# A permuted table for the ranks within a block of a mixture-of-experts layer

## The chip, the cores and the metric

The kernel runs on one core of a Trainium2 chip. The metric is the device time of one execution in microseconds (us). The core has TensorE (PE), VectorE (DVE), ScalarE (ACT), GpSimd (POOL) and SyncE (SP), and 16 DMA engines that move data between the chip's memory (HBM) and the on-chip SBUF.

## The reference

Two transformer blocks on 512 tokens of width 1024, in float32. The change touches only the last sublayer, a mixture of 32 experts of which each token takes two. Cut to that:

```python
weights = p_grp[:, None] * top_p / jnp.sum(top_p, axis=-1, keepdims=True)
expert_id = grp[:, None] * EXPERTS_PER_GROUP + top_e
...
order = jnp.argsort(flat_e)
...
def run_block(args):
    xb, e, wb = args
    a = jax.nn.silu(xb @ w_gate[e]) * (xb @ w_up[e])
    return (a @ w_down[e]) * wb[:, None].astype(xb.dtype)
...
y = jnp.zeros((T, D), h.dtype).at[slot_tok].add(out.reshape(cap, D))
```

The 1024 pairs of token and expert (512 tokens, `TOP_K` 2) are grouped by expert; each expert's rows go through gate, up and down; the results are added back to their tokens. In which order the rows of one expert stand does not matter to the result.

## The kernel before

The program runs the first transformer block, the second block's mixer, and then the routing and the experts. One instruction stream for each engine is written out by hand, with semaphores between them.

**Routing** (VectorE, lines 2010 to 2099). For each pair the kernel computes a slot: a block number and a rank within a block of `BS` = 64. The first 64 tokens of expert e go to block e (32 blocks), the rest of experts with more than 64 tokens to overflow blocks after them. `dst_r` is the rank, `dst_b` the start of the block. Two one-hot tables are made by comparison: `block_tok` (line 2077, block against all blocks, then multiplied by the token's number) and `place` (line 2079, rank against the table `iota_r`, which holds 0 to 63). TensorE multiplies the two (line 2790), so that row p, column b of the product says which token stands on partition p of block b; the same matmul is done for both halves of 64 partitions. From it come `slot_i`, the index of the row to gather, and `pair_i`, the index of the row to scatter to. A spot with no token gets an index out of bounds.

```python
dve.tensor_tensor(place, cols(tab3, TAB3, "iota_r").unsqueeze(1).to_broadcast([P, 8, BS]),
                  dst_r.unsqueeze(2).to_broadcast([P, 8, BS]), ALU.is_equal).then_inc(S("places_ready"), 1)
```

**The experts.** For each block b, GpSimd gathers up to 64 rows of 4 KB from `xn_rows` in HBM into 64 partitions of `raw` (`gather`, line 865, four blocks ahead). TensorE turns them (line 2818), VectorE scales and shifts them (lines 2107, 2109), TensorE computes gate and up (`gate_up`, line 2802, 32 matmuls), ScalarE and VectorE form the activation (lines 1300 to 1308, 2114, 2116), TensorE turns it and computes down (`down`, line 2810), VectorE multiplies the result (line 2123), and GpSimd scatters it to `y_rows` in HBM (`scatter`, line 870). A result row of 4 KB is scattered as two rows of 2 KB, since `down` leaves its left half on partitions 0 to 63 and its right half on 64 to 127: 128 rows in each scatter. The order on TensorE is: gate_up(b), turn and down of b - 1, rows of b + 2.

```python
pool.indirect_dma_start(xg(v), None, xn_rows, bass.IndirectOffsetOnAxis(ap=index, axis=0),
                        bounds_check=T - 1, oob_is_err=False).then_inc(S(f"xg_loaded{v}"), 16)
```

**The weights** (SP, `expert_gu` line 627 with 2 MB for gate and up, `expert_dn` line 631 with 1 MB for down) go into seven slots. The load of block b + 7 is issued when gate_up(b), or down(b), is done. The two overflow blocks take the same way in a loop at the end (lines 728 and 731). After the last scatter SP loads `y_rows` (line 742), and the four tiles of 128 tokens are summed, normed and stored.

**Tables.** `routing_tables` (lines 1979 to 1988) prepares constants on VectorE between the two halves of the output projection, where it follows the operations of lines 1997 and 1999.

Of the kernel before, what the change touches and what calls it, by code (L numbers as in the profile page):

```python
# [26 lines left out]
P = 128  # L27
# [41 lines left out]
BS = 64  # L69
# [34 lines left out]
def columns(fields):  # L104
    at, out = 0, {}
    for name, n in fields:
        out[name] = (at, at + n)
        at += n
    out["_"] = (0, at)
    return out  # L110
# [5 lines left out]
TAB3 = columns([("dec", 32), ("iota", NBLK), ("thr", 8), ("tok", 2 * NT), ("iota_r", BS), ("iota_b", NBLK + 2), ("final_g", D)])  # L116
# [162 lines left out]
def build(nc, x, wp, par_d, con_d, smw_d, bias_d, par2_d, smw2_d, tab2_d, tab3_d, wexp, out):  # L279
    with ExitStack() as ctx:  # L280
# [5 lines left out]
        def S(name):  # L286
            if name not in sems:
                sems[name] = ctx.enter_context(nc.semaphore(name))
            return sems[name]
# [32 lines left out]
        def AR(a, n):  # L322
            return arena[:, a:a + n]

        def cols(t, table, name):
            a, b = table[name]
            return t[:, a:b]
# [149 lines left out]
        tab3 = AR(14848, TAB3_N)  # L477
# [3 lines left out]
        def AT(n):  # L481
            at[0] += n
            assert at[0] <= 18560
            return AR(at[0] - n, n)
# [21 lines left out]
        place = AR(12288, 8 * BS).rearrange("p (c n) -> p c n", c=8)  # L506
# [6 lines left out]
        half_of = AT(1)  # L513
        dst_i = AT(8).bitcast(I32)
        idxc, idxp = AT(WS).bitcast(I32), AT(WS).bitcast(I32)
        nblkf = AT(1)
        nblk_i = AT(1).bitcast(I32)
        actf = AT(2 * P).rearrange("p (u n) -> p u n", u=2)
# [24 lines left out]
        def wait_group(eng, what, i):  # L543
            eng.wait_ge(S("group_filled"), GIDX[what, i] + 1)
            return BANKS[WHERE[GIDX[what, i]]]
# [787 lines left out]
        def _(dve):  # L1333
            c = [0]

            def own(ins):
                c[0] += 1
                ins.then_inc(S("dve_step"), 1)
                dve.wait_ge(S("dve_step"), c[0])
# [64 lines left out]
            for c4 in range(4):  # L1404
                b = wait_group(dve, "cT", c4)
# [228 lines left out]
            for t in range(len(units) + 3):  # L1634
# [14 lines left out]
                if t == len(units) + 1:  # L1649
                    b = wait_group(dve, "csq", 0)  # L1650
# [46 lines left out]
            for r in range(FQ):  # L1697
                for j in range(4):
                    if m < MOD_PIECES:
                        mod_part(m)  # L1700
                    for f in range(2):
                        i = (r * 4 + j) * 2 + f
# [7 lines left out]
                for j in range(4):  # L1710
# [15 lines left out]
                    for t in range(NT if j % 2 else 0):  # L1726
                        i = (r * 2 + half) * 4 + t
                        xt = Xv[:, t, half * 512:(half + 1) * 512]
                        b = wait_group(dve, "down", i)
# [40 lines left out]
            b = wait_group(dve, "if", 0)  # L1770
            free_group(dve.tensor_copy(if_rows, b[0:8, :]), "if", 0)
            b = wait_group(dve, "ifT", 0)
# [7 lines left out]
            b = wait_group(dve, "lb", 0)  # L1780
# [26 lines left out]
            b = wait_group(dve, "cum", 0)  # L1807
# [3 lines left out]
            for h in range(MH):  # L1811
                b = wait_group(dve, "crow", h)
# [63 lines left out]
            for i in range(8):  # L1876
                b = wait_group(dve, "bm", i)
# [8 lines left out]
            for f in range(5):  # L1886
                b = wait_group(dve, "cT2", f)
# [17 lines left out]
            b = wait_group(dve, "krT", 0)  # L1905
# [3 lines left out]
            for t in range(NT):  # L1909
                b = wait_group(dve, "qr", t)  # L1910
# [8 lines left out]
            for t in range(NT):  # L1919
                b = wait_group(dve, "qrT", t)  # L1920
# [29 lines left out]
            for t in range(len(aunits) + 5):  # L1950
# [6 lines left out]
                if t >= 11 and (t - 11) % 8 < 2:  # L1957
                    q, i = divmod(t - 11, 8)
                    b = wait_group(dve, "yaT", 2 * q + i)
# [7 lines left out]
            for i in range(8):  # L1967
# [4 lines left out]
                b = wait_group(dve, "ba", i)  # L1972
# [6 lines left out]
            def routing_tables():  # L1979
                dve.wait_ge(S("tables_loaded"), TABLES["tab3"])  # L1980
                dve.tensor_copy(tri_r, cols(con, CON, "tri"))
                dve.tensor_copy(one_r, one.to_broadcast([P, 2]))
                dve.tensor_scalar(second[:, 0:4], cols(tab3, TAB3, "tok")[:, 0:4], -8.0 * T, None, ALU.add)
                dve.tensor_scalar(second[:, 4:8], cols(tab3, TAB3, "tok")[:, 4:8], -7.0 * T, None, ALU.add)
                dve.memset(half_of[0:BS, :], 16.0 * T)
                dve.memset(half_of[BS:P, :], 16.0 * T + 1)
                dve.memset(slot_i.bitcast(F32), float(T))
                dve.tensor_tensor(triex[0:32, :], cols(con, CON, "tri")[0:32, 0:32], ident[0:32, 0:32], ALU.subtract)

            wait_freed(dve, "g1r", 1)  # L1990
            dve.wait_ge(S("x_back"), 16)
            for half in range(2):
                for t in range(NT):
                    i = 4 * half + t
                    b = wait_group(dve, "wout", i)
                    w = wtmp[:, i % 2, :]
                    own(dve.tensor_tensor(w, b[:, :], g1row[:, half * 512:(half + 1) * 512], ALU.mult))
                    xt = Xv[:, t, half * 512:(half + 1) * 512]
                    free_group(dve.tensor_tensor(xt, xt, w, ALU.add), "wout", i)
                if half == 0:  # L2000
                    routing_tables()
# [3 lines left out]
            for n in (5, 7):  # L2005
                b = wait_group(dve, "xT", n)
# [15 lines left out]
            b = wait_group(dve, "gr", 0)  # L2022
            free_group(dve.tensor_copy(gr_rows[0:100, :], b[0:100, 0:256]), "gr", 0)
            b = wait_group(dve, "grT", 0)
# [27 lines left out]
            b = wait_group(dve, "cnt", 0)  # L2052
# [4 lines left out]
            b = wait_group(dve, "rank", 0)  # L2057
            free_group(dve.tensor_tensor(Sl, b[:, 0:128].rearrange("p (t n) -> p t n", t=NT), Aa.bitcast(F32), ALU.subtract), "rank", 0)
            b = wait_group(dve, "pstart", 0)
# [8 lines left out]
            for A, k in ((A1, 0), (A2, 1)):  # L2068
# [7 lines left out]
            iota_b = cols(tab3, TAB3, "iota_b").unsqueeze(1).to_broadcast([P, 8, NBLK + 2])  # L2076
            own(dve.tensor_tensor(block_tok, iota_b, dst_b.unsqueeze(2).to_broadcast([P, 8, NBLK + 2]), ALU.is_equal))
            own(dve.tensor_tensor(block_tok, block_tok, second.unsqueeze(2).to_broadcast([P, 8, NBLK + 2]), ALU.mult))
            dve.tensor_tensor(place, cols(tab3, TAB3, "iota_r").unsqueeze(1).to_broadcast([P, 8, BS]),
                              dst_r.unsqueeze(2).to_broadcast([P, 8, BS]), ALU.is_equal).then_inc(S("places_ready"), 1)  # L2080
            b = wait_group(dve, "slots", 0)
            own(dve.tensor_scalar(slot_f[:, 0:NBLK + 2], b[:, 0:NBLK + 2], -7.0 * T, -float(T), ALU.is_ge, ALU.mult))
# [54 lines left out]
            with dve.Fori(0, OVER // WS) as i:  # L2137
                for v in range(WS):
                    b, u = NE + WS * i + v, v % 2
# [901 lines left out]
```

## Time and profile before

| | |
|---|---|
| Time, median of 3 runs | 1604.31 us (1603.09 to 1606.16) |
| The profiled execution, its own time | 1599.82 us |
| Its span, first to last instruction | 1598.0 us |
| Granted TensorE clock, mean | 0.981 |
| Busy: PE, DVE, ACT, POOL | 1503.4, 782.5, 454.9, 588.3 us |
| DMA over the whole span | 260.92 MB, mean 163 GB/s |

How to read the profile: times are microseconds from the start of the span unless marked ns. PE is TensorE's matmuls and PEld its weight loads. Busy is the time in which an engine executes. The DMA share is the mean busy share of the 16 DMA engines (measured packet by packet, so it can come out a little above 1), and GB/s is what they moved. "issue" as a releaser means that the engine waited for nothing that the profile shows. A transfer is cut into packets; queue q1 holds the plain loads and stores that SP issues, q0 the gathers and scatters that GpSimd issues. The completion of a transfer is itself one small packet on each of the 16 engines.

### The profile page before, as it was taken

The numbers are of one execution on the slowest core, as the hardware profiler recorded it, in microseconds if no ns is written. First come the engines' busy times: TensorE is split into PE (matmuls) and PEld (weight loads), VectorE is DVE, ScalarE is ACT, GpSimd is POOL, SyncE is SP. The second block draws the span as 40 slices with busy tenths as digits, with TensorE's granted clock in tenths as the row PEclk, the third lists the DMA queues.
The fourth block names the chain that finished last, engine by engine and source line by source line (L and its number), as shares of the span: only waits on it lengthen the run. The fifth ranks groups of instructions, "written<-read, shape, count | busy, mean of one in ns | idle before, by whom it ended". The sixth has DMA issues, their size and how long they took to land.

```text
span 1598.0 us, 21257 instructions
## 1 busy us (share of the span) xinstructions
PE 1503.4 (94%) x8338; PEld 1188.7 (74%) x8338; DVE 782.5 (49%) x1490; ACT 454.9 (28%) x734; POOL 588.3 (37%) x486
## 2 busy tenths in 40 slices
PE   7999999999999999999999999999999989977885
PEld 6978887878888888877888988775788766544442
DVE  5475657387786863245605602445313354432334
ACT  4342334342222313252414332442223211100001
POOL 5551222434545444553533154510254313321222
PEclk9999999999999999999999999999999999988898
DMA  4250110335445442222322022310143799999995
GB/s 174 104 199 27 53 54 1 132 132 199 170 179 190 182 161 105 105 113 79 112 79 80 27 83 102 115 54 1 43 169 139 302 354 365 370 397 367 394 409 208
DMA packets 37348, 260.92 MB, mean 163 GB/s; under 512 B 7280, under 2 KB 7920, under 8 KB 13184
## 3 DMA queue, kind: packets, MB, share of 16 engines
q1 hardware_dynamic: 31488, 251.13, 41.4%
q0 software_dynamic: 5760, 8.41, 1.7%
q8 instruction: 68, 1.11, 0.3%
q14 instruction: 32, 0.26, 0.0%
HBM read 252.69 MB, written 17.30 MB: 169 GB/s over the span
## 4 chain that ended last, share of the span: by engine, by line
PE 83%; DVE 6%; issue 5%; ACT 2%; POOL 2%; DMA 1%; DVEq 0%; SPq 0%; ACTq 0%; POOLq 0%
PE G L2214 13%; PE G L2216 12%; PE G L2215 12%; PE SA L2802 4%; PE G L2802 4%; PE SA L2214 3%; PE SA L2216 3%; PE SA L2215 3%; PE PB L2216 3%; PE PB L2215 3%; PE PB L2214 3%; PE OB L2411 2%; POOL wl L770 1%; PE PB L2810 1%; PE SA L2682 1%
## 5 line engine op out<-in xcount | busy, mean ns | idle before, releaser
L770 POOL TENSOR_TENSOR wl<-raw,wh 128x512 fp32r<-128x512 f32 x352 | 476.3, 1385 | 676.0 <-ACT wh L925 666.3
L925 ACT ACTIVATE wh<-raw 128x2048 fp32r<-128x2048 f32 x90 | 172.3, 1914 | 270.9 <-PE SA L2216 142.6
L2214 PE MATMUL G<-Hh,wh 128*128 128x512 f32 x544 | 216.4, 398 | 2.6 <-DVE arena L1617 1.4
L2216 PE MATMUL G<-Hh,wl 128*128 128x512 f32 x544 | 212.8, 391 | 0.0
L2215 PE MATMUL G<-Hl,wh 128*128 128x512 f32 x544 | 212.4, 391 | 0.0
L1694 DVE SCALAR_TENSOR_TENSOR arena<-arena,st 128x256 f32<-128x256 f32 x144 | 132.9, 923 | 5.1
L2214 PEld LDWEIGHTS G<-Hh,wh 128*128 128x128 f32 x544 | 102.5, 188 | 23.4 <-issue 2.2
L2216 PEld LDWEIGHTS G<-Hh,wl 128*128 128x128 f32 x544 | 102.4, 188 | 22.2
L2215 PEld LDWEIGHTS G<-Hl,wh 128*128 128x128 f32 x544 | 102.6, 189 | 19.5
L865 POOL DMA_INDIRECT raw<-xn_rows,arena x38 | 36.6, 963 | 131.2 <-PE G L2818 107.5
L2214 PE MATMUL G<-wh,Hh 128*128 128x256 f32 x256 | 77.6, 303 | 1.1 <-POOL wl L770 1.0
L2216 PE MATMUL G<-wh,Hl 128*128 128x256 f32 x256 | 72.9, 285 | 0.0
L2215 PE MATMUL G<-wl,Hh 128*128 128x256 f32 x256 | 72.9, 285 | 0.0
L2214 PE MATMUL G<-Yh,wh 128*128 128x512 f32 x168 | 65.6, 390 | 1.6 <-DVE Yl L1890 1.6
L870 POOL DMA_INDIRECT y_rows<-arena x34 | 34.4, 1013 | 87.2 <-DVE arena L2123 82.3
L1011 ACT ACTIVATE arena<-arena,st 128x128 f32<-128x128 f32 (+3 forms) x64 | 35.9, 561 | 103.8 <-DVE st L1576 103.8
L2216 PE MATMUL G<-Yh,wl 128*128 128x512 f32 x168 | 65.4, 389 | 0.0
L2215 PE MATMUL G<-Yl,wh 128*128 128x512 f32 x168 | 65.4, 389 | 0.0
L1585 DVE COPY arena<-PB 128x128 f32<-128x128 f32 (+3 forms) x64 | 31.3, 489 | 49.2 <-PE PB L2401 48.8
L2214 PE MATMUL SA<-wh,Yh 128*128 128x512 f32 x134 | 53.6, 400 | 0.0
L2214 PEld LDWEIGHTS G<-wh,Hh 128*128 128x128 f32 x256 | 49.4, 193 | 4.1 <-issue 1.7
L2216 PE MATMUL SA<-wh,Yl 128*128 128x512 f32 x134 | 52.4, 391 | 0.0
(535 smaller groups left out, 3087.4 us busy)
## 6 DMA issues: line engine op xcount, KB each, us to landing
raw<-in_pieces_dram SPq DMA_DIRECT2D x91, 1024.0 KB, 4.8
arena<-in_pieces_dram SPq DMA_DIRECT2D x24, 1024.0 KB, 4.8
arena<-in_wexp_dram SPq DMA_DIRECT2D x11, 2048.0 KB
dn_w<-in_wexp_dram SPq DMA_DIRECT2D x18, 1024.0 KB
arena<-in_wexp_dram SPq DMA_DIRECT2D x12, 1024.0 KB, 26.9
gu_y<-in_wexp_dram SPq DMA_DIRECT2D x6, 2048.0 KB
gu_z<-in_wexp_dram SPq DMA_DIRECT2D x5, 2048.0 KB, 43.3
gu_h<-in_wexp_dram SPq DMA_DIRECT2D x4, 2048.0 KB, 37.1
```

The costliest lines, as they stand in the source:

```text
L770: ins = pool.tensor_tensor(low_[:, part], whole[:, part], high[:, part], ALU.subtract)
L865: pool.indirect_dma_start(xg(v), None, xn_rows, bass.IndirectOffsetOnAxis(ap=index, axis=0), bounds_check=T - 1, oob_is_err=False).then_in ...
L870: pool.indirect_dma_start(y_rows, bass.IndirectOffsetOnAxis(ap=index, axis=0), yb[:, u, :], None, bounds_check=4 * T - 1, oob_is_err=False ...
L925: act.activation(split_pair(s)[0], wait_raw(act, sp_list[s]), ACT.Copy).then_inc(S("high_split"), 1)
L1011: act.activation(SP[:, u % 2, 0:nk], SP[:, u % 2, 0:nk], ACT.Exp, scale=-1.0, bias=nmax[:, u % 2:u % 2 + 1], accum_out=rsum[:, ((u // 8) % ...
L1585: dve.tensor_copy(PTs[:, u % 2, 0:nk], PB[u % 2][:, 0:nk]).then_inc(S("pt_copied"), 1)
L1694: own(dve.scalar_tensor_tensor(a, w[:, k, :], condc[:, k:k + 1], a, ALU.mult, ALU.add))
L2214: pe.matmul(out, ah, bh, start=first, stop=False)
L2215: pe.matmul(out, ah, bl, start=False, stop=False)
L2216: return pe.matmul(out, al, bh, start=False, stop=last)
L2411: ins = pe.matmul(OB[:, h * HD:(h + 1) * HD], PTs[:, u % 2, k * P:(k + 1) * P], Zv[:, k, ty, (h // 4) * HD:(h // 4 + 1) * HD], start=k == ...
L2802: ins = pe.matmul(GU[u][BS * j:BS * j + BS, 0:256], xgT[:, u, k, :], wg[:, j, k, :], start=k == 0, stop=k == KT - 1)
```

## The change

A second table of 64 numbers, `rank_at`, is built once from `iota_r` and takes its place in the comparison that makes `place`. It holds a permutation of 0 to 63: with a rank written in bits as (b, c, j, i), where i has three bits and the others one each, the rank stands at position (c, i, j, b). So ranks 0 to 7 stand at positions 0, 4, 8, ... 28; ranks 8 to 15 at 2, 6, ... 30; ranks 16 to 31 at the even positions from 32 on; and ranks 32 to 63 at the odd ones. A token of rank r is then found at that partition of its block, in the gather and in the scatter alike. Nothing else is changed.

```diff
@@ -513,6 +513,7 @@
         half_of = AT(1)
         dst_i = AT(8).bitcast(I32)
         idxc, idxp = AT(WS).bitcast(I32), AT(WS).bitcast(I32)
+        rank_at = AT(BS)
         nblkf = AT(1)
         nblk_i = AT(1).bitcast(I32)
         actf = AT(2 * P).rearrange("p (u n) -> p u n", u=2)
@@ -1985,6 +1986,11 @@
                 dve.memset(half_of[0:BS, :], 16.0 * T)
                 dve.memset(half_of[BS:P, :], 16.0 * T + 1)
                 dve.memset(slot_i.bitcast(F32), float(T))
+                ranks = cols(tab3, TAB3, "iota_r").rearrange("p (b c j i) -> p b j c i", b=2, c=2, j=2)
+                spots = rank_at.rearrange("p (c i j b) -> p b j c i", c=2, j=2, b=2)
+                for j in range(2):
+                    for b in range(2):
+                        dve.tensor_copy(spots[:, b, j], ranks[:, b, j])
                 dve.tensor_tensor(triex[0:32, :], cols(con, CON, "tri")[0:32, 0:32], ident[0:32, 0:32], ALU.subtract)
 
             wait_freed(dve, "g1r", 1)
@@ -2076,7 +2082,7 @@
-            dve.tensor_tensor(place, cols(tab3, TAB3, "iota_r").unsqueeze(1).to_broadcast([P, 8, BS]),
+            dve.tensor_tensor(place, rank_at.unsqueeze(1).to_broadcast([P, 8, BS]),
                               dst_r.unsqueeze(2).to_broadcast([P, 8, BS]), ALU.is_equal).then_inc(S("places_ready"), 1)
```

On VectorE the four copies stand behind the constants of `routing_tables`, in the middle of the output projection (`arena` is the large work area, `con` the constants, SA and PB banks of PSUM). Before:

```order
L1987 MEMSET arena 128x52
L1988 TENSOR_TENSOR arena<-con 32x32
L1997 TENSOR_TENSOR arena<-SA,arena 128x512
L1999 TENSOR_TENSOR X<-X,arena 128x512
```

And now:

```order
L1988 MEMSET arena 128x52
L1993 COPY arena<-arena 128x16 x4
L1994 TENSOR_TENSOR arena<-con 32x32
L2003 TENSOR_TENSOR arena<-SA,arena 128x512
L2005 TENSOR_TENSOR X<-X,arena 128x512
```

Four copies of 16 elements on 128 partitions are new; the rest keeps its order, six lines further down in the file. No other engine has an instruction more or less.

## Rows read from the trace of the kernel before

**Rows 1.** Chain that ended last, gate and up: start us, us, what.
```profile
1354.22 3.45 PE G L2802 x32
1360.30 3.45 PE SA L2802 x32
...
1537.25 3.67 PE G L2802 x32
1544.98 3.67 PE SA L2802 x32
1553.88 3.47 PE G L2802 x32
```

**Rows 2.** Stretches: us, busy of PE, PEld, DVE, ACT, POOL, PEclk, DMA share, GB/s.
```profile
1350.00:1380.00 30.00, 29.91 (x250) 18.42 (x248) 14.12 (x25) 3.27 (x10) 9.86 (x10) 1.00 1.01 381
...
1500.00:1530.00 30.00, 22.15 (x154) 13.41 (x156) 9.13 (x17) 1.96 (x6) 6.93 (x7) 0.87 1.01 402
1530.00:1550.00 20.00, 18.26 (x144) 11.17 (x142) 5.91 (x11) 1.96 (x6) 2.99 (x3) 0.94 1.00 418
```

**Rows 3.** PE line 2802 from 1390 to 1546: idle before it, by releaser (us, times).
```profile
  issue: 29.1, 13
```

**Rows 4.** Stretches of 2 us at the end of the weight stream.
```profile
1556.00:1558.00 2.00, 2.00 (x23) 1.44 (x18) 0.14 (x1) 0.38 (x1) 0.98 (x4) 1.00 0.92 383
1558.00:1560.00 2.00, 0.94 (x8) 0.59 (x8) 1.90 (x4) 0.28 (x1) 0.70 (x1) 1.00 0.78 322
1560.00:1562.00 2.00, 2.00 (x14) 0.99 (x12) 0.40 (x2) 0.00 (x0) 0.00 (x0) 1.00 0.53 215
1562.00:1564.00 2.00, 2.00 (x22) 1.60 (x20) 0.47 (x1) 0.00 (x0) 0.67 (x1) 1.00 0.42 174
1564.00:1566.00 2.00, 1.90 (x20) 1.25 (x15) 0.38 (x1) 0.38 (x1) 0.34 (x1) 1.00 0.35 131
1566.00:1568.00 2.00, 1.04 (x7) 0.68 (x9) 1.84 (x4) 0.28 (x1) 0.00 (x0) 1.00 0.17 70
1568.00:1570.00 2.00, 1.39 (x8) 0.25 (x4) 0.47 (x1) 0.00 (x0) 0.31 (x2) 1.00 0.13 41
1570.00:1572.00 2.00, 0.00 (x0) 0.00 (x0) 0.22 (x1) 0.00 (x0) 0.99 (x1) 1.00 0.00 0
```

**Rows 5.** Stretches of 1 us at the end of the y_rows loads.
```profile
1587.00:1588.00 1.00, 1.00 (x4) 0.30 (x2) 0.96 (x2) 0.00 (x0) 0.91 (x2) 1.00 0.56 229
1588.00:1589.00 1.00, 0.37 (x1) 0.00 (x0) 0.84 (x1) 0.59 (x3) 0.92 (x2) 1.00 0.02 8
```

**Rows 6.** DMA queues and issues of the whole program: packets, MB; issues.
```profile
q0 software_dynamic: 5760, 8.41, 1.7%
...
raw<-xn_rows,arena POOLq DMA_INDIRECT x38
y_rows<-arena POOLq DMA_INDIRECT x34
```

**Rows 7.** DMA packets from 1502.3 to 1503.1 (two rows), then to 1506.0.
```profile
DMA packets 51, 0.32 MB, mean 405 GB/s; under 512 B 19, under 2 KB 19, under 8 KB 26
q0 software_dynamic: 25, 0.03, 11.4%
...
q0 software_dynamic: 80, 0.03, 3.7%
```

**Rows 8.** DVE in order of time: start us, us, line, operation, [idle before].
```profile
1251.82 0.16 DVE L1984 TENSOR_SCALAR arena<-arena 128x4 f32<-128x4 f32 x1
...
1264.08 0.69 DVE L1997 TENSOR_TENSOR arena<-SA,arena 128x512 f32<-128x512 f32 x1 [11.79 <-PE SA L2216]
...
1294.94 0.69 DVE L2079 TENSOR_TENSOR arena<-arena 128x512 f32<-128x512 f32 x1
```

**Rows 9.** Chain that ended last: the first gather.
```profile
1298.35 4.54 DMA raw<-xn_rows,arena
```

**Rows 10.** DMA packets from 1315 to 1545.
```profile
DMA packets 12059, 87.89 MB, mean 382 GB/s; under 512 B 3722, under 2 KB 3722, under 8 KB 5515
```

## The prediction

> **What bounds the kernel now.** I read the busy shares by stretch first, then the chain, then the DMA views. The stage that matters is the expert loop, from about 1307 us to the end: 32 blocks of 64 ranks, one for each expert, then two overflow blocks. The reader should see four things.
>
> The loop has two paces. Early, the gate-and-up groups follow each other at 1354.22, 1360.30 us: 6.08 us a block, with TensorE busy throughout [rows 1, 2]. Late they start at 1537.25, 1544.98 and 1553.88: 7.7 us and more [rows 1], and TensorE is busy only 22.15 of 30 us [rows 2]. From 1390 to 1546 it stands idle 29.1 us ahead of these groups for nothing that the profile shows [rows 3]. The group waits for rows, for a free buffer and for its weights. The first two come from engines that the view would name; what is left is the weight load.
>
> The DMA engines are busy all the time: share 1.01 in both paces and 1.00 up to 1550 [rows 2]. So the stream of weights sets the late pace, and what counts is when the last gate-and-up load (block 31) is complete.
>
> A load is complete when the slowest of its 16 engines is done, and the engines are far from each other. At the end of the stream the share falls 0.92, 0.78, 0.53, 0.42, 0.35, 0.17, 0.13 over windows of 2 us from 1556 on [rows 4]. That is one engine after another running dry, over 14 us. The sum is 3.30, so the mean engine ends 6.6 us after 1556, and the last near 1570, 14 us after it: **the slowest is 7.4 us behind the mean**. The y_rows loads later, with no row transfers among them, end sharply: 0.56, then 0.02 a microsecond later [rows 5]. So the engines are not unequal as such. Something between 1300 and 1556 drove them apart.
>
> **What drives them apart.** The only transfers there that need not be even are the gathers and the scatters: 38 and 34, 8.41 MB [rows 6]. Absent ranks are skipped: 1024 assignments of 4 KB, gathered and scattered, are just 8.39 MB. Packets tell how rows are laid out. The gather of block 31, with 8 tokens, is 80 packets: 64 rows and 16 completions. Its packets between 512 B and 8 KB number 26 less 19, that is 7, in the first 0.8 us [rows 7]; at most one more can follow. The whole program has 5760 such packets [rows 6]. 38 x 64 gathered rows, 72 x 16 completions and 34 x 128 scattered rows would be 7936; with scattered rows in twos it is 2432 + 1152 + 2176 = 5760, exactly. Rows that share a packet share an engine, so neighbouring ranks do lie together, and low ranks, which nearly every expert has, load always the same engines. The single packet records, which no view groups, fit twos for the gather and fours for the scatter (low half rows on one set of eight engines, high half rows on the other).
>
> The reference's routing gives the tokens of each expert: 5 to 89, two of them above 64. With that placement I added up bytes by engine. Before, the heaviest engine has 252 KB more than the mean over all 34 blocks, and 219 KB when block 31's weights land (32 gathers, 28 scatters). With permuted ranks it has 72 and 65 KB.
>
> **The change part by part.**
> - Four copies of 128x16 on VectorE. The nearest rows are 0.16 us for 128x4 and 0.69 us for 128x512 [rows 8]; I take 0.2 us each, 0.8 us in all. They stand where VectorE is then idle for 11.79 us, waiting for TensorE [rows 8]. Even at 0.69 each, 2.8 us are covered. Cost: 0. Without that cover it would be the 0.8.
> - The comparison reads another table of the same shape: 0.69 us as now [rows 8]. Cost: 0.
> - The same 1024 ranks are matched, so bytes, numbers of transfers, of turns on GpSimd and of matmuls stay. The first gather, 4.54 us on the chain [rows 9], has 25 tokens: at most two rows per engine either way. Cost: 0; I keep 0.3 us to either side.
> - Evenness of the engines. An engine moves 418/16 = 26.1 GB/s [rows 2]. 252 KB are then 9.7 us, where the decline shows 7.4: the trace gives 0.77 of the arithmetic. At block 31 the lead of the heaviest falls by 219 - 65 = 154 KB, 5.9 us, times 0.77: **-4.5 us**. The ends are 0 (the skew has another cause) and -7.4 (perfect evenness). I take 4.5, since it is held to the decline.
> - Scattered rows. The even spots now hold ranks 0 to 31 and the odd ones 32 to 63, so a packet of two mostly has one present rank and one absent. Packets with data go from 1040 to 1624. Their number with and without data is unchanged, and so are the bytes. No row prices this. The lower bound is 0. For the upper one: 87.89 MB between 1315 and 1545 [rows 10] would take 210.3 us at 418 GB/s and take 230, so 19.7 us are lost; were all of that the price of scatter packets with data, 584/1040 more would cost 11.1 us. I take 0, as share and bytes say that engines never stand.
>
> Sum: -4.5 us. Behind block 31's start nothing else comes due: from 1544.98 to the end are 53 us of TensorE, VectorE and final loads that move along. The loads of blocks 32 and 33 are behind in the same queues and gain as much. Next late after the weights is TensorE itself at 6.08 us a block, which is well below 7.7. The execution profiled took 1599.8 us (span 1598.0) and would take 1595.3; it stands 4.5 us below the median of 1604.3, so I set the median at **1599.8**.
>
> The Trainium skill (DMA: Bandwidth & Descriptors, "The descriptor swizzle") places partitions of a 128-partition transfer in fours over eight engines for each half. For the scatter this is my placement. If the 64-row gather followed it too, all gathers would load eight engines, and by that rule the heaviest would be some 620 KB above the mean, 23 us, going down to 12: a gain of 9 us or more. The decline of 7.4 us disagrees, and so does the burst of seven rows in 0.8 us.
>
> **The rivals.**
> - *The slow engines are always the same ones*, whatever the ranks: some port or ring is slow during row transfers. For it: the skew is there only while they run. Against it: a few slow engines would give a fall to a low step; rows 4 show a steady fall over all 16. Ranks would not matter: 1604.3. The Trainium skill (same page, "Latency and other measured facts") says that engines 7 and 15 are usually slower, perhaps through ring traffic of GpSimd's transfers. By that rule the share would drop to 2/16 = 0.13 and stay; only the last two windows look so. Chance 0.20, with the case that the change spreads ranks otherwise than I think.
> - *The half-filled scatter packets cost time* (the other sign). Place: each engine's queue from 1310 to 1550. If the 19.7 us lost go by all row packets (1024 + 1040), 584 more cost 5.6 us: net +1.1, 1605.4. If by the scatter's alone, 11.1: net +6.6, 1610.9. It decides once a further packet costs its engine 4.5 x 16 / 584 = 0.12 us. Against it: each engine's number of turns is the same. Chance 0.12.
> - *More evenness than I count*: the lag of 7.4 us goes nearly whole: 1597. Chance 0.08.
>
> **How the numbers follow.** The forecast has 0.60, its own range 1598.4 to 1601.5. About 0.2% (3.2 us) is what a measurement can tell from no change. Faster: 0.56 of the forecast's 0.60 and the 0.08 of more evenness, 0.64. Same: 0.04, 0.18 of the first rival, 0.03 of the second: 0.25. Slower: 0.09 of the second and 0.02: 0.11. The range runs from 1595 (evenness plus 2 us between runs) to 1606, past the mild form of the second rival; outside lie its strong form and little else.
>
> **What would show it.** Right: the share at the stream's end falls from about 1 to below 0.2 within some 5 us instead of 14; the last gate-and-up groups start 4 to 5 us earlier measured from the first one; the early pace stays 6.08 us; the idle time ahead of them falls by about as much; GB/s between 1315 and 1545 stays near 382. Wrong: a decline as long as before (first rival), or a sharp one with lower GB/s and equal or later groups (second). Four copies that delay the next operation on VectorE would refute the cover.

## The result, and the profile after

| | before | after |
|---|---|---|
| Time, median of 5 runs each | 1605.43 us (1603.09 to 1607.32) | 1595.99 us (1592.56 to 1598.23) |
| Profiled execution: own time, span | 1599.82, 1598.0 us | 1593.49, 1591.6 us |
| First gather to the end of the span | 299.6 us | 290.3 us |

The ratio is 0.9928, with a 95% interval of 0.9911 to 0.9945. By these medians the kernel is 9.4 us faster, where the forecast said 4.5: the direction is right, and the gain is twice as large. The time of 1596.0 lies in the stated range, near its lower end.

The two profiled executions differ before the routing as well: the first gather is issued at 1298.35 us before and at 1301.36 after. A third execution, of the kernel before, had it at 1304.5, and its expert loop took 299.6 us again. So that offset varies from one execution to another, and everything below is measured **from the first gather on**.

The chain that ended last, of after: the first gather, two early gate-and-up groups, the group of block 31 (start us, us, what; line 2808 is line 2802 of before).

```profile
1301.36 4.42 DMA raw<-xn_rows,arena
...
1351.10 3.45 PE SA L2808 x32
1357.17 3.45 PE G L2808 x32
...
1538.37 3.67 PE SA L2808 x32
```

The early pace is 6.08 us a block, as before [rows 1]. The group of block 31 starts at 1538.37, that is 237.0 us after the first gather; before it was 1544.98 - 1298.35 = 246.6 [rows 1, 9]. It comes 9.6 us sooner, and the end comes 9.3 us sooner. So the whole gain is there when block 31 starts, and what lies behind it only moves along.

Stretches of after, 3 us later than those of [rows 2] and 1 us later than those of [rows 4], with the same columns.

```profile
1353.00:1383.00 30.00, 29.91 (x250) 18.39 (x247) 14.13 (x25) 3.26 (x10) 9.84 (x10) 1.00 1.01 388
1503.00:1533.00 30.00, 23.62 (x176) 14.36 (x174) 10.60 (x19) 1.96 (x6) 7.47 (x8) 0.94 1.01 413
1533.00:1553.00 20.00, 17.20 (x136) 10.32 (x132) 7.98 (x15) 2.24 (x7) 4.28 (x6) 1.00 1.01 423
...
1555.00:1557.00 2.00, 2.00 (x22) 1.57 (x20) 0.69 (x1) 0.00 (x0) 0.27 (x1) 1.00 1.01 420
1557.00:1559.00 2.00, 2.00 (x21) 1.44 (x18) 0.00 (x0) 0.38 (x1) 0.73 (x1) 1.00 0.79 326
1559.00:1561.00 2.00, 0.93 (x10) 0.69 (x10) 1.89 (x4) 0.28 (x1) 0.00 (x0) 1.00 0.62 244
1561.00:1563.00 2.00, 1.79 (x8) 0.39 (x6) 0.41 (x2) 0.00 (x0) 0.23 (x2) 1.00 0.20 72
1563.00:1565.00 2.00, 0.00 (x0) 0.00 (x0) 0.62 (x1) 0.00 (x0) 1.07 (x2) 1.00 0.01 4
```

Two things have changed. First, the engines now run dry within about 6 us instead of 14. The shares from 1557 on sum to 1.62, so the mean engine ends at 1557 + 3.2 = 1560.2, and the last near 1563: 2.8 us behind the mean, where it was 7.4. Second, the share is 1.01 as before, but the engines move more in the same busy time: 388 GB/s for 381, 413 for 402, 423 for 418. The mean engine ends 1560.2 - 1301.4 = 258.9 us after the first gather; before it was 1562.6 - 1298.35 = 264.3. **By these shares the lag of the slowest engine gave 4.6 us and the rate of all of them 5.4.** Together that is 10.0, where the group of block 31 came 9.6 sooner. The single arrivals, used further down, give 4.7 and 5.0.

For the rate I take the same stretch in each kernel, 190 us long, from 16.65 us after the first gather. Packets in it, before and after:

```profile
DMA packets 9961, 71.52 MB, mean 376 GB/s; under 512 B 3135, under 2 KB 3135, under 8 KB 4655
```

```profile
DMA packets 10214, 73.32 MB, mean 386 GB/s; under 512 B 2734, under 2 KB 2734, under 8 KB 4784
```

The change moves 1.80 MB more in 190 us, which is 4.3 us of work at 418 GB/s. It also has fewer packets under 512 B, since a pair of scattered rows is now absent as a whole less often. The records of single packets show it: in these 190 us 942 packets of the change carry 2052 bytes, a row of 2048 and 4 bytes for the absent one. So the scattered rows do go in twos. In the whole program q0 has 5760 packets and 8.41 MB, as before [rows 6].

TensorE's idle time ahead of the gate-and-up groups, after, 1393 to 1549 us:

```profile
  issue: 21.4, 9
  DVE arena L2115: 9.1, 7
```

The wait for weights fell from 29.1 us [rows 3] to 21.4. The wait for the rows' scale and shift on VectorE rose to 9.1 us, from 4.7 before:

```profile
  DVE arena L2109: 4.7, 3
```

So the two together fell by only 3.3 us, although the group of block 31 starts 9.6 us sooner. Where the weights come earlier, the rows are next to be late.

The four copies on VectorE, after (columns as in [rows 8]):

```profile
1255.19 1.46 DVE L1993 COPY arena<-arena 128x16 f32<-128x16 f32 x4
...
1267.08 0.69 DVE L2003 TENSOR_TENSOR arena<-SA,arena 128x512 f32<-128x512 f32 x1 [9.25 <-PE SA L2222]
```

They take 1.46 us, and 9.25 us of idle time for TensorE are left behind them. They cost nothing.

### The profile page after: what moved, and what is told of

Read it like the earlier page. It is cut to its first block, busy times and chain, and to the rows that moved or that the text cites. A ratio compares the mean times of both kernels' runs of the same rounds, so it can differ in the third digit from the quotient of the medians.

```text
span 1591.6 us, 21261 instructions
## 1 busy us (share of the span) xinstructions
PE 1499.3 (94%) x8338; PEld 1187.4 (75%) x8338; DVE 783.7 (49%) x1494; ACT 455.0 (29%) x734; POOL 588.0 (37%) x486
## 3 DMA queue, kind: packets, MB, share of 16 engines
q0 software_dynamic: 5760, 8.41, 1.6%
## 4 chain that ended last, share of the span: by engine, by line
PE 83%; DVE 6%; issue 5%; ACT 2%; POOL 2%; DMA 1%; DVEq 0%; SPq 0%; ACTq 0%; POOLq 0%
PE G L2220 13%; PE G L2222 12%; PE G L2221 12%; PE SA L2808 4%; PE G L2808 4%; PE SA L2220 3%; PE SA L2222 3%; PE SA L2221 3%; PE PB L2222 3%; PE PB L2220 3%; PE PB L2221 3%; PE OB L2417 2%; POOL wl L771 1%; PE SA L2688 1%; PE G L2268 1%
```

## The experiments

That the lead of the heaviest engine, added up over the blocks, delays the last engine is common to all theories. They differ in why the whole stream became faster. The expectations call them by numbers:

- **Theory 1**: the rate follows the same added-up lead, so a kernel whose engines stay level is also faster on the mean.
- **Theory 2**: the rate follows how rows lie in packets and on even or odd partitions.
- **Theory 3**: the rate follows how many engines share the rows of one transfer. In **3a** that of the gather counts, in **3b** that of the scatter.

"Density" below means how few engines the rows of one transfer fall on.

The tables. "Mean" is when block 31's gate and up weights arrive, averaged over the 16 engines; "lag" is how much later the last engine is. Both are read from the records of single arrivals, which no view groups. "MB" is from the packets of the 190 us named above. "Lead" is the heaviest engine's bytes above the mean at block 31, added up from the routing with the placement inferred in the prediction, for 32 gathers and 28 scatters. (The gathers of blocks 32 and 33, 41 rows, are in fact done by then too. With them 219 KB become 225, and 65 become 67.) The times in us are from the first gather, and each row is one trace, while the ratios of whole times come from 4 to 12 executions.

| kernel | end | mean | lag | MB | lead, KB | ratio of times, 95% |
|---|---|---|---|---|---|---|
| before | 299.6 | 239.5 | 7.1 | 71.52 | 219 | |
| before again (e12) | 299.6 | 238.7 | 6.5 | 71.69 | 219 | |
| the change | 290.3 | 234.5 | 2.4 | 73.32 | 65 | 0.9928 [0.9911, 0.9945] |
| e1 table only | 290.9 | 235.3 | 2.5 | 73.06 | 65 | 0.9946 [0.9934, 0.9958] |
| e2 half-filled | 302.9 | 238.8 | 7.9 | 71.85 | 219 | 1.0001 [0.9991, 1.0011] |
| e3 most uneven | 316.2 | 240.9 | 19.8 | 71.03 | 499 | 1.0091 [1.0078, 1.0104] |
| e4 before, mirrored | 293.4 | 237.2 | 2.5 | 72.17 | 33 | 0.9976 [0.9966, 0.9985] |
| e5 change, mirrored | 292.4 | 235.4 | 2.2 | 72.82 | 12 | 0.9935 [0.9914, 0.9957] |
| e6 pairs, mirrored | 295.0 | 236.7 | 1.8 | 72.50 | 26 | 0.9973 [0.9956, 0.9990] |
| e7 worst, mirrored | 299.2 | 240.9 | 3.5 | 71.09 | 82 | 1.0000 [0.9986, 1.0014] |
| e11 quads, mirrored | 295.6 | 237.6 | 2.7 | 72.29 | 57 | one execution |

**e1, the table alone.** The permutation is made by the host, and VectorE copies nothing.

```diff
- _rows(np.arange(BS))
+ _rows(np.arange(BS).reshape(2, 2, 2, 8).transpose(1, 3, 2, 0).reshape(-1))
```

> The changed kernel's table, laid down with the constants instead of by four VectorE copies. Both theories: the same as the change, ratio to before near 0.993, the share at the end of the weight stream falling within 7 us, and the copies worth under 0.5 us. It is the baseline of the other three.

Measured: 1597.31 us beside 1605.82 of before; the loop takes 290.9 us, with the change 290.3. The order of the ranks does it, and the copies cost nothing that can be measured.

**e2, half-filled packets with the engines' load as before.** The permutation only splits ranks 0 to 31 from 32 to 63 within a pair: 1624 scatter packets with data, as in the change, and the lead of before.

```diff
+ _rows(np.arange(BS).reshape(2, 16, 2).transpose(2, 1, 0).reshape(-1))
```

> Another table: every engine gets exactly the bytes of before (heaviest 219 KB above the mean at block 31), but ranks r and r+32 share a packet and rows lie on even partitions first, as in the change (1624 scatter packets with data). Theory 1, evenness alone, and the higher rate comes from the engines staying in step: as before, ratio 0.998 to 1.002, decline over 14 us, 382 GB/s from 1315 to 1545. Theory 2, the higher rate comes from how rows lie in packets and partitions: ratio near 0.997 (5 us less), about 389 GB/s, decline still over 14 us. The rival of the prediction, half-filled packets cost: ratio above 1.001.

Measured: 1606.39 us, ratio 1.0001. Packets of the 190 us:

```profile
DMA packets 9991, 71.85 MB, mean 378 GB/s; under 512 B 2691, under 2 KB 2691, under 8 KB 4662
```

The packets under 512 B fell to 2691, so the edit did what it says; bytes, mean and lag stayed. Its one trace takes 302.9 us from the first gather, 3.3 more than before, but over 11 executions nothing of that is left. The rival of half-filled packets falls: at 11.1 us, or at 5.6, this kernel would show it. Theory 2 falls with it, since it wanted 5 us less. The run also bears out the twos of the gather. Were its rows dealt out in fours over all 16 engines, the same sum over the routing would give a lead of 366 KB before and 211 in e2, yet the lags are 7.1 and 7.9 us.

**e3, the most uneven table.** Four neighbouring ranks share an engine in the gather, eight in the scatter.

```diff
+ _rows(np.arange(BS).reshape(16, 2, 2).transpose(1, 0, 2).reshape(-1))
```

> Another table: four neighbouring ranks on each engine in gather and scatter, so that the heaviest engine is 499 KB above the mean at block 31 (219 before), with full packets (1040 with data). By bytes at 26.1 GB/s times 0.77 the lag at block 31 is 14.7 us against 6.4, so 8.3 us later than before. Theory 1: more, since the rate falls with the skew: 13 to 18 us later, ratio 1.008 to 1.011, under 378 GB/s. Theory 2: 8 us later, ratio 1.005, and 382 GB/s.

Measured: 1620.62 us, ratio 1.0091. Stretches at the end of its weight stream:

```profile
1581.00:1583.00 2.00, 1.78 (x8) 0.38 (x6) 0.41 (x2) 0.00 (x0) 0.00 (x0) 1.00 0.22 90
1583.00:1585.00 2.00, 1.56 (x14) 1.09 (x16) 0.61 (x1) 0.00 (x0) 0.53 (x1) 1.00 0.17 66
1585.00:1587.00 2.00, 2.00 (x20) 1.19 (x16) 0.00 (x0) 0.00 (x0) 0.48 (x1) 1.00 0.17 66
1587.00:1589.00 2.00, 1.34 (x14) 1.08 (x12) 1.29 (x3) 0.38 (x1) 0.00 (x0) 1.00 0.12 51
```

The share falls to 0.17 and stays near it: two or three engines carry the rest for some 8 us. The lag of block 31's weights is 19.8 us with a lead of 499 KB, 7.1 with 219 and 2.4 with 65. The place of the ranks sets how far the slow engines fall behind, and the rival by which they are slow whatever the ranks falls too. The kernel is 14.8 us slower than before, as Theory 1 wanted, but not for its reason: the mean arrival is only 1.8 us later (240.9 for 239.1, the mean of two traces of before), and the lag 13.0 (19.8 for 6.8).

The lag also grows along the stream, as a lead that adds up over the blocks must make it. In the records of single arrivals it is 2.4 us for the load that lands 35 us after the first gather, 5.6 at 118 us and 7.1 at 239 in the kernel before; in e3 it is 5.9, 14.9 and 19.8 at about the same places; with the change it is 1.7, 1.6 and 2.4.

**e4, e5: mirrored.** In every second block the ranks are counted from the other end (63 for 0), so the lead almost vanishes while the rows within one transfer stand as densely as without the mirror. e4 does it on the table of before, e5 on the change's.

```diff
+ own(dve.tensor_scalar(dst_ri[:, :], dst_i[:, :], 2 * BS - 1, None, ALU.bitwise_and))
+ own(dve.tensor_copy(dst_r, dst_ri[:, :]))
+ own(dve.tensor_scalar(dst_f, dst_r, -1.0, 2.0 * BS - 1, ALU.mult, ALU.add))
+ own(dve.tensor_tensor(dst_r, dst_r, dst_f, ALU.min))
```

> The table of before, but ranks of odd blocks are counted from the other end (63 minus rank), by four more small VectorE operations (some 0.8 us on the routing path). Neighbours still share packets (1040 with data) and lie on neighbouring partitions, while the heaviest engine is only 33 KB above the mean at block 31. Theory 1: as good as the change but for the 0.8 us, ratio 0.992 to 0.994, about 389 GB/s. Theory 2: only the evenness, 4.5 to 6 us less the 0.8, ratio 0.997, 382 GB/s.

> The changed table and, in odd blocks, ranks counted from the other end: the heaviest engine is only 12 KB above the mean at block 31 (65 in the change), and each single transfer is spread as in the change. From the first gather to the end the change takes 290.3 us, its lag at block 31's weights is 2.4 us. Both theories: the lag falls to about 1 us. Theory 1 (the rate follows the skew between engines over the whole stream): mean arrival of those weights 234 after the first gather as in the change, end 289. Theory 3 (the rate follows how many engines share the rows of one transfer): the same, 289. Whole time: the 0.8 us of the four small operations is given back, so ratio 0.993 to 0.995.

Measured: 1601.72 and 1597.45 us. The four operations stand ahead of the first gather and cost 0.8 us there. e4 has the change's lag, 2.5 us, but only about half of its gain in the mean: 237.2, against 239.1 of before (two traces) and 234.9 with the table of the change (the change and e1). By the packets of the 190 us it is a third, 0.57 of 1.59 MB. Its ratio, 0.9976, is outside what Theory 1 wanted. So evenness over the blocks is not all of it, and the rest depends on how rows stand within a transfer. e5 has no advantage over the change itself, and its loop ends at 292.4 us where 289 was expected. Its lag stays at 2.2 us where 1 was expected: some 2 us of lag don't come from the lead.

**e6, e7, e11: other tables, mirrored.** With the lead small in all, they differ in how densely the rows of one transfer stand. By the placement, the heaviest engine's bytes above the mean, summed over the single transfers, are (gathers, scatters, in KB): change 49 and 22, pairs 131 and 49, before 131 and 121, quads 295 and 121, worst 295 and 287.

```diff
pairs: .reshape(2, 2, 8, 2).transpose(0, 2, 1, 3)
quads: .reshape(2, 8, 2, 2).transpose(2, 1, 0, 3)
worst: .reshape(16, 2, 2).transpose(1, 0, 2)
```

> Mirrored, with a table that leaves the gather as in e4 (two neighbours on an engine) but spreads the scatter's rows over twice as many engines, in twos where e4 has fours. Skew over the stream 26 KB, as low as in e4 (33). Theory 1: as e4, mean arrival 237.2 us after the first gather, end 293.4. Theory 3: between e4 and the change, mean arrival about 235.8, end 291.5 to 292.5.

> Mirrored, with e3's table: every transfer loads as few engines as can be (four ranks each), while the skew over the stream is 82 KB, near the change's 65. Theory 1: mean arrival near 235 to 237, end near 293. Theory 3: the mean arrival is at least as late as before's 239.5 and near e3's 240.9, end near 297.

> Mirrored; four neighbouring ranks on one engine in the gather (as e7), but in the scatter only as dense as in e4. Skew 57 KB. Theory 3a (the gather's spread sets the rate): mean arrival as in e7, 240 to 241, end near 298.5. Theory 3b (the scatter's): as in e4, 237, end near 294. Theory 1: 236 to 237.

Measured: 1600.96, 1605.70 and 1605.32 us. The means, in order of density: 235.4 (e5), 236.7, 237.2 (e4), 237.6 and 240.9 us. The clearest is e7, with 10 executions: its lead is near the change's, and yet it gains nothing on before, ratio 1.0000. That refutes Theory 1, which wanted a mean of 235 to 237. The mean rises with density, but not with that of the gather alone: quads has a gather more than twice as dense as e4's and is only 0.4 us later, less than the 0.8 us by which two traces of the same kernel differ, where 3a wanted 240 to 241. e6 lies between its two theories, too near both to decide.

**e8, e9, e10: no rows.** e8 scatters nothing (all indices out of bounds; `y_rows` is filled with weights early), e9 gathers nothing, e10 neither.

```diff
e8:
- dve.memset(half_of[0:BS, :], 16.0 * T)
+ dve.memset(half_of[0:BS, :], 32.0 * T)
e9:
- ... b[:, 0:NBLK + 2], 8.0 * T, slot_f ...
+ ... b[:, 0:NBLK + 2], 16.0 * T, slot_f ...
```

> The kernel before with all scatter indices out of bounds, so that no result row is written (y_rows is filled once, early, with other numbers); the gathers are as they were. The 4.19 MB not moved are 0.6 us per engine per megabyte, 10.0 us at 418 GB/s. Theory 1: the skew left is the gather's, 125 of 219 KB; the mean arrival falls by the bytes, 8.5 us by block 31, and 1 to 2 more for the smaller skew: about 229. Theory 3, with the scatter as the main cost: more than that, 225 or less.

> The kernel before with all gather indices out of bounds: no row is read into the blocks, which compute on what lies there; scatters as before. Without 3.9 MB by block 31, 9.4 us of bytes at 418 GB/s go from the mean arrival of its weights (239.5 us after the first gather). With the scatter's rows left out (e8) it came 6.7 us earlier, less than their 8.4 us of bytes. Theory 3a, the gather's rows are what makes the others' packets longer: over 11 us earlier, under 228, and weight packets' excess well below before's 20.7 us per engine. Theory 1: 9 to 10 us, about 230.

> Both left out (no row gathered, none scattered). Bytes: 17.8 us less, mean arrival 221.7. Theory 3a: 217 or less, the weights stream near 418 GB/s. Theory 1: the same, as there is no skew left. If the stream stays near 380 GB/s, rows are not what slows it at all, and both fall. The lag at block 31 falls to 1 us.

Measured in one execution each: 1602.96, 1570.15 and 1566.29 us. (In e8 the first gather is issued only at 1308.5 us, so its whole time hides what the loop gained.) Packets of the 190 us in e9:

```profile
DMA packets 11531, 79.37 MB, mean 418 GB/s; under 512 B 4472, under 2 KB 4472, under 8 KB 5360
```

Without gathered rows the stream moves 418 GB/s over these 190 us, and the mean arrival comes at 209.4 us, 29.7 sooner than before. The rows left out are 4.2 MB, all 1024 of them, 10.0 us at 418 GB/s. So **the gathered rows cost three times their bytes**. Without scattered rows the mean comes at 232.8, 6.3 us sooner, for 3.6 MB, 8.6 us of bytes: they cost no more than their bytes. All theories had both runs wrong: they wanted 229 or less for e8 and 228 to 230 for e9. With neither (e10) it comes at 202.6, 6.8 us before e9, so that holds without the gathers as well. The 19.7 us by which the stream falls short of 418 GB/s belong to the gathers.

Where the time goes can be read from the queues. Packets, MB and share of the 16 engines' time in the 190 us, of before, then the weights' queue of after, then e9:

```profile
q1 hardware_dynamic: 5948, 65.13, 90.7%
q0 software_dynamic: 3998, 6.19, 10.3%
```

```profile
q1 hardware_dynamic: 6086, 66.62, 90.7%
```

```profile
q1 hardware_dynamic: 6925, 75.53, 94.6%
q0 software_dynamic: 4589, 3.60, 5.7%
```

The gathers' own packets are not what is dear: q0 has 10.3% with them and 5.7% without, 8.7 us of 190. The weights' packets take longer. In e9 75.53 MB of them take 179.7 us of each engine. At that price the 65.13 MB of before would take 155.0 us, and they take 172.3: **17.3 us more, twice the gathers' own time**. With the change the same sum gives 13.8 us more for 66.62 MB, and the 3.5 us between the two are most of the 4.3 that it gained here. The records of single packets show the same. A weight packet of 16 KB takes 684 ns on the mean before, 678 with the change and 616 in e9, one of 8 KB 355, 337 and 317 ns, while the medians hardly differ (619, 619 and 613 ns for 16 KB). So most packets are untouched and some are much longer, and those stand where rows are moved. In e8, which has gathered rows only, a 16 KB packet takes 624 ns on the mean where no row packet starts in its microsecond, and 850 where 10 to 19 do.

**e12** is the kernel before, unchanged, to show how far two traces of one kernel differ. It took 1606.03 us, and its mean arrival came 0.8 us sooner than that of the first trace.

> The kernel before, unchanged, once more with its trace. All theories: from the first gather to the end 299.6 us, mean arrival of block 31's weights 239.5 us after the first gather, lag 7.1; how far it is off tells what differences of single traces are worth. The first gather itself can move by several us between executions.

**e13 to e16: which transfer must be spread.** The change's table with the edit of e8 (e13) and of e9 (e14), and e8 and e9 once more on the same chip (e15, e16). One execution each: 1601.34, 1577.34, 1597.69 and 1573.41 us.

> The change's table, and no row is scattered (the index of every row is out of bounds; y_rows is filled with other data early). To be read against the same edit on the kernel before (232.8 us from the first gather to the mean arrival of block 31's gate/up weights, 238.1 to the last). Rate from the gathers' spread: mean about 4 us earlier, 228 to 229.5. Rate from the scatters' spread: mean unchanged, 232 to 233.6. Both by halves: about 230.5. In every case the lag of the last engine falls, from 5.3 to about 2 us.

> The change's table, and no row is gathered (indices out of bounds). To be read against the same edit on the kernel before (209.4 us to the mean arrival, 212.2 to the last, first gather to end 267.4). Rate from the gathers' spread: mean unchanged, 208.6 to 210.2. Rate from the scatters' spread: mean about 4 us earlier, near 205.5. Lag falls by about 1 us in every case (121 KB of scatter skew at 0.77 of 26.1 GB/s are 3.6 us, of which 2.8 show; 23 KB are left).

> The kernel before without scattered rows, once more, as the partner of the run with the change's table on the same chip. Every theory: within 0.8 us of the earlier look, 232.8 us to the mean arrival of block 31's weights, lag 5.3 us. If it differs by more, single looks can't part the theories.

> The kernel before without gathered rows, once more, as the partner of the run with the change's table on the same chip. Every theory: within 0.8 us of the earlier look, 209.4 us to the mean arrival of block 31's weights, lag 2.7 us.

**e17, e18:** as e15 and e13, mirrored. One execution each: 1600.62 and 1595.31 us.

> The table of before, every second block mirrored (ranks counted from the other end), and no row scattered. Each gather is as dense on its engines as before (131 KB above its mean in sum), but over the blocks the engines are loaded evenly. Mean arrival of block 31's weights after the first gather was 232.8 and 232.9 us with this table unmirrored and 228.8 with the change's. If unevenness that adds up over the blocks costs rate: near 228.8, lag about 2.5. If the density of each gather costs rate: stays at 232.9, lag about 2.5. Between them: both.

> The change's table, every second block mirrored, and no row scattered. Density of each gather as with the change (49 KB), added-up unevenness smaller still. Added-up unevenness costs rate: mean a little below 228.8, by at most 47/125 of the 4.1 us that the table gave, so 227.3 to 228.8. Density costs rate: 228.8 within 0.4. Both theories: lag 2 to 2.6.

| rows left | table | end | mean | lag | MB |
|---|---|---|---|---|---|
| gathers | before (e8, e15) | 292.6, 290.2 | 232.8, 232.9 | 5.3, 4.9 | 70.87, 70.90 |
| gathers | change (e13) | 285.9 | 228.8 | 2.6 | 72.06 |
| gathers | before, mirrored (e17) | 290.7 | 231.5 | 2.9 | 71.31 |
| gathers | change, mirrored (e18) | 287.8 | 229.1 | 2.4 | 71.99 |
| scatters | before (e9, e16) | 267.4, 268.8 | 209.4, 209.6 | 2.7, 3.0 | 79.37, 79.28 |
| scatters | change (e14) | 266.1 | 207.5 | 2.3 | 79.83 |

The repeats agree within 0.2 us in the mean. With only the gathers there, the change's table gives 4.1 us in the mean (232.9 to 228.8). With only the scatters it gives 2.0 (209.5 to 207.5). Both theories of a single transfer are too simple: the gathers carry the larger part, the scatters a smaller one, and the two don't add up (6.1 us apart, 4.2 together). e17 and e18 split the gathers' gain: taking away the unevenness over the blocks alone gives 1.4 us (232.9 to 231.5), and spreading the rows within each gather gives another 2.4 (231.5 to 229.1). With all rows there the split is 1.9 (239.1 to e4's 237.2) and 1.8 (to e5's 235.4). These differences are only two to three times the 0.8 us of noise. They have a bias besides: the mirrored kernels start their first gather some 0.8 us later, while the weights loaded ahead of it come as early as before, so times from the first gather flatter them a little. The packets of the 190 us put the evenness lower, at 0.42 MB of e13's 1.17, 1.0 us of work at 418 GB/s.

The lags say once more that gathered rows weigh more than scattered ones. By the placement the gathers alone have a lead of 125 KB before and the scatters alone 94 KB. The lags are 5.3 and 4.9 us with the one, 2.7 and 3.0 with the other, hardly more than the 2 us that are always there.

## Why the prediction was half right

- **What bounds the kernel: right.** Weights ending last at block 31 set the end. The group of block 31 came 9.6 us sooner and the end 9.3.
- **The engines driven apart by the places of the ranks: right,** and shown by e2, e3 and e4: the lag goes with the lead in KB (1.8 to 3.5 us at 12 to 82 KB, 6.5 to 7.9 at 219, 19.8 at 499), and some 2 us are left where the lead is almost nothing.
- **"Evenness of the engines", -4.5 us: right for what it counted, in part by luck.** The lag fell by 4.6 us by the shares and by 4.7 (or 4.1 against the second trace) by the arrivals. The factor 0.77 came out here, 4.1 to 4.7 for 5.9 us of arithmetic, but it is no constant. From 219 to 499 KB, 10.7 us by the arithmetic, the lag rose by 13.0 (e3). And the 7.4 us that it was taken from hold some 2 us that don't come from the lead.
- **Four copies, 0: right.** I took 0.2 us each; together they were 1.46 us, within the 2.8 that were bounded, under the same cover. The comparison and the first gather cost nothing either.
- **Half-filled scatter packets, 0: right,** shown by e2.
- **The step that failed** is the assumption under the same heading, "Evenness of the engines", that only the slowest engine's distance from the mean would shrink, put at the end as "GB/s between 1315 and 1545 stays near 382". It rose: to 391 GB/s in that window, and from 71.52 to 73.32 MB in equal stretches. The mean arrival came 5.0 us sooner in the two profiled executions, 4.2 with two traces of each table. That is the part of the gain that the forecast had left out. I had seen that 19.7 us were lost against 418 GB/s, but asked only whether the change would add to them, through the scatter. They came from the gathers, whose rows make the weights' packets longer (e9), and rows that are spread lose less. The term of the sum should have been some -9, and the range should have reached below 1595 on that account. The prediction had no row that showed this: it took a run without gathered rows to see it.
- **The rival of slow engines that are always the same: wrong.** The Trainium skill (DMA: Bandwidth & Descriptors, "Latency and other measured facts") has engines 7 and 15 as usually slower. By that rule the share of after would have dropped to 0.13 and stayed; it went 0.62, 0.20, 0.01.
- **The placement in fours for the gather too, and a gain of 9 us or more: right number, wrong cause.** The Trainium skill (DMA: Bandwidth & Descriptors, "The descriptor swizzle") gives that placement for a transfer to 128 partitions. Taken for the 64-row gather, it would have left a lag of 12 us by the prediction's estimate. The measured lag is 2.4, so the gather's rows lie otherwise.
- **The rival "more evenness than I count"** named the size (1597) but not the cause: the lag did not go whole, 2.4 us are left.
- **Groups "start 4 to 5 us earlier": wrong for the same reason,** 9.6. The early pace and the shorter decline (some 6 us where 5 were said) came true.

What stays open: gathered rows in flight make the weights' packets longer, but what in the chip does it, and why spread rows do it less, was not found. Nor is the measure of density found. e3 and e7 have equally dense transfers and very different leads, and the same mean (240.9), while e4 gained 1.9 us in the mean by a smaller lead alone. The tables e4 and e11 differ twofold in the gather's density and hardly in the mean. The decompositions above rest on one or two traces each, where those of one kernel differ by 0.8 us. No table was found that beats the change.

## What to carry to other kernels

Where a weight stream sets the pace, look at how it ends: a DMA share that fades over several us says that some engines carry more than others, and the gathers and scatters beside it are the first to ask, since their rows fall on engines by partition. Ask separately when the mean engine is done and how far the slowest is behind it, for a change of layout can move both. And when a share of 1.01 stands beside less than the best GB/s of the same program, find out which transfers take that rate away before any term of the sum assumes that it stays.

## What the runs showed of the hardware

- Rows gathered from HBM by index slow the plain loads beside them: 376 GB/s with them, 418 without (e9), at a busy share near 1.01 in both. 4.2 MB of gathered rows cost 29.7 us, 3.6 MB of scattered rows 6.3 (e8).
- The cost lies in the other queue: a 16 KB weight packet takes 684 ns on the mean beside the gathers and 616 without (e9), with nearly the same median.
- The same bytes, gathered and scattered by the same number of transfers, gave 71.0 to 73.3 MB in 190 us, depending only on which partitions held the rows (e3 and the change).
- The slowest of the 16 engines completed block 31's weights 19.8 us behind their mean where the ranks gave it 499 KB more than the mean, 7.1 us at 219 KB and 1.8 to 2.7 at 12 to 65 KB.
